# Reloads in the up rounds issued from the scalar engine's queue, and two loops of up rounds written out

## What is computed

```
experts, gates = top-k over two sets of 128 keys, softmax      # 128 experts a position
hdn = gelu(einsum('ted,td->te', expert_down[experts], x))
y   = einsum('te,ted->td', gates * hdn, expert_up[experts])
```

## Time and profile before

| | us |
|---|---|
| median of 3 runs | 3018.91 |
| lowest and highest | 3017.72, 3021.58 |
| the profiled execution: its time | 3036.75 |
| the profiled execution: its span | 3034.7 |

### The profile page before, as it was taken

How to read it: one execution, slowest core, us unless ns; L and a number is a source line. 1 busy time by engine, 2 the same in 40 slices (tenths; PEclk the granted TensorE clock), 3 DMA queues, 4 the chain that set the end, 5 groups by cost and what they waited for, 6 DMA issues and landing times.

```text
span 3034.7 us, 44598 instructions
## 1 busy us (share of the span) xinstructions
PE 2999.1 (99%) x16703; PEld 2676.0 (88%) x16703; DVE 1970.3 (65%) x2549; ACT 1473.1 (49%) x1794; POOL 945.9 (31%) x675
## 2 busy tenths in 40 slices
PE   9999999999999999999999999999999999999998
PEld 8999888888888888998999999999878888888887
DVE  5445564688875555687988976645776555555554
ACT  6445454555564444544444444554555434444443
POOL 3110000088888887155777840000000000000000
PEclk9999999999999999999999999999999999999999
DMA  7764467577777778898999985654446666666664
GB/s 228 246 205 140 147 216 253 187 210 204 213 204 203 225 209 260 296 334 308 351 363 351 349 308 193 191 180 136 132 146 187 192 191 193 191 191 193 190 193 153
DMA packets 227280, 672.30 MB, mean 222 GB/s; under 512 B 57116, under 2 KB 60838, under 8 KB 226737
## 3 DMA queue, kind: packets, MB, share of 16 engines
q1 hardware_dynamic: 157696, 549.79, 55.5%
q0 software_dynamic: 63680, 103.36, 11.8%
q10 hardware_dynamic: 5744, 16.99, 1.5%
HBM read 631.85 MB, written 38.12 MB: 221 GB/s over the span
## 4 chain that ended last, share of the span: by engine, by line
PE 95%; DVE 2%; issue 1%; ACT 1%; DMA 1%; ACTq 0%; SPq 0%; DVEq 0%
PE ps L1954 14%; PE ps L2248 10%; PE ps L2095 8%; PE ps L2097 8%; PE ps L2096 8%; PE ps L1933 8%; PE ps L1934 8%; PE ps L1932 8%; PE ps L1953 7%; PE ps L2247 5%; PE ps L1950 1%; PE ps L2261 1%; PE ps L2260 1%; PE ps L2262 1%; DVE w_lo L691 1%
## 5 line engine op out<-in xcount | busy, mean ns | idle before, releaser
L691 DVE TENSOR_TENSOR w_lo<-raw,w_hi 128x1024 fp32r<-128x1024 f32 (+2 forms) x1072 | 1274.0, 1194 | 855.7 <-ACT w_hi L686 801.1
L686 ACT ACTIVATE w_hi<-raw 128x1024 fp32r<-128x1024 f32 (+2 forms) x1072 | 1107.4, 1034 | 1274.0 <-PE ps L1934 338.4
L1954 PE MATMUL ps<-x_all,w_hi 128*128 128x512 f32 x1920 | 667.7, 390 | 0.0
L1953 PE MATMUL ps<-x_all,w_lo 128*128 128x256 f32 x1920 | 541.7, 282 | 2.3 <-DVE w_lo L691 2.3
L551 POOL DMA_INDIRECT gates<-srch x256 | 486.4, 1900 | 160.5 <-issue 78.5
L2248 PE MATMUL ps<-acts,w_hi 128*128 128x416 f32 x1680 | 514.4, 370 | 3.7 <-issue 3.7
L2247 PE MATMUL ps<-acts,w_lo 128*128 128x208 f32 x1680 | 437.7, 261 | 5.3 <-issue 4.9
L2095 PE MATMUL ps<-w_hi,x_all 128*128 128x440 f32 (+2 forms) x1152 | 436.4, 379 | 0.4 <-DVE w_lo L691 0.4
L1954 PEld LDWEIGHTS ps<-x_all,w_hi 128*128 128x128 f32 x1920 | 360.5, 188 | 74.6
L2096 PE MATMUL ps<-w_lo,x_all 128*128 128x440 f32 (+2 forms) x1152 | 424.7, 369 | 0.0
L2097 PE MATMUL ps<-w_hi,x_all 128*128 128x440 f32 (+2 forms) x1152 | 424.7, 369 | 0.0
(11 more groups left out here) (390 smaller groups left out, 3522.4 us busy)
## 6 DMA issues: line engine op xcount, KB each, us to landing
raw<-in_peer_down SPq DMA_DIRECT2D x256, 512.0 KB
raw<-in_peer_up SPq DMA_DIRECT2D x256, 512.0 KB
raw<-in_w_mlp_in SPq DMA_DIRECT2D x128, 512.0 KB
raw<-in_w_mlp_out SPq DMA_DIRECT2D x128, 512.0 KB
raw<-in_w_in SPq DMA_DIRECT2D x112, 440.0 KB
raw<-in_w_in SPq DMA_DIRECT2D x96, 428.0 KB
raw<-in_w_out SPq DMA_DIRECT2D x64, 512.0 KB
gates<-zero POOLq DMA_DIRECT2D x32, 512.0 KB, 4.9
```

The costliest lines, as they stand in the source:

```text
L686: act.activation(w_hi[:, c % RING, 0:2 * n], raw[:, c % RING, 0:2 * n], ACT.Copy).then_inc(hi_made, 1)
L691: nc.vector.tensor_tensor(w_lo[:, c % RING, 0:2 * n], raw[:, c % RING, 0:2 * n], w_hi[:, c % RING, 0:2 * n].bitcast(F32), ALU.subtract).th ...
L1953: mm(o[:, 0], wl, xh, start=False, stop=False)
L1954: last = mm(o, wh, both, start=False, stop=(k == KT - 1))
```

## The change

GpSimd keeps the reloads of the first four blocks, counted by four new semaphores `first_loaded`. Its other 28 pairs go to ScalarE's queue: `bring_next(nu, g)` is called after the `split_hi` of chunks 9, 11, 13 and 15 of up round nu (block 1, odd chunks) for nu = 0 to 6, and brings block 4(nu + 1) + g. It waits for the same `hid_lo` count, but no longer for `spilled`. GpSimd then has the sets alone, one after the other, held only by `rows_used`; sets 0 to 2 come before its wait for all of `spilled`, as three did. VectorE's `fill` waits for `first_loaded` in its first round and counts one less later. TensorE's and ScalarE's loops over up rounds 1 to 6 become Python loops, so six copies of the body stand in the program. No arithmetic changes.

```diff
-SETS_BY = (3, 7, 15, 22, 29, 36, 44, 48)
...
             def bring(m):
 
-                buf = m % RING
-                if m >= RING:
-                    pool.wait_ge(hid_lo, m - RING + 1)
                 pool.wait_ge(spilled, 16 * (m + 1))
-                pool.dma_start(hid_ring[:, buf].rearrange("p (j s) -> p j s", j=JJ), hid_dense[m, :, :, 0:TD]).then_inc(reloaded[buf], 16)
-                pool.dma_start(gat[:, buf].rearrange("p (j s) -> p j s", j=JJ), gates_dense[m, :, :, 0:TD]).then_inc(gates_loaded[buf], 16)
+                pool.dma_start(hid_ring[:, m].rearrange("p (j s) -> p j s", j=JJ), hid_dense[m, :, :, 0:TD]).then_inc(first_loaded[m], 16)
+                pool.dma_start(gat[:, m].rearrange("p (j s) -> p j s", j=JJ), gates_dense[m, :, :, 0:TD]).then_inc(first_loaded[m], 16)
...
-            done = 0
-            for r in range(PEER_ROUNDS):
-                if r == 1:
-                    pool.wait_ge(pieces_made, 4)
-                    while done < SETS_BY[0]:
-                        gather_rows(done)
-                        done += 1
-                for g in range(RING):
-                    bring(4 * r + g)
-                if r == 1:
+            for m in range(RING):
+                bring(m)
+            pool.wait_ge(pieces_made, 4)
+            for s in range(SETS):
+                if s < GBUF - 1:
+                    gather_rows(s)
+                if s == GBUF - 1:
                     pool.wait_ge(spilled, 16 * 4 * PEER_ROUNDS)
-                    for s in range(done):
-                        gather_hidden(s)
-                while r and done < SETS_BY[r]:
-                    gather_rows(done)
-                    gather_hidden(done)
-                    done += 1
+                    for before in range(s):
+                        gather_hidden(before)
+                if s >= GBUF - 1:
+                    gather_rows(s)
+                    gather_hidden(s)
...
+            def bring_next(nu, g):
+
+                m = 4 * (nu + 1) + g
+                act.wait_ge(hid_lo, m - RING + 1)
+                act.dma_start(hid_ring[:, g].rearrange("p (j s) -> p j s", j=JJ), hid_dense[m, :, :, 0:TD]).then_inc(reloaded[g], 16)
+                act.dma_start(gat[:, g].rearrange("p (j s) -> p j s", j=JJ), gates_dense[m, :, :, 0:TD]).then_inc(gates_loaded[g], 16)
...
+                        if up and i == 1 and c % 2 and nu < PEER_ROUNDS - 1:
+                            bring_next(nu, c // 2)
...
-            with act.Fori(1, PEER_ROUNDS - 1) as r:
+            for r in range(1, PEER_ROUNDS - 1):
                 phase(True, PEER_ROUNDS, r, True, True)
...
-                dve.wait_ge(gates_loaded[g], 16 * (f + 1))
-                dve.wait_ge(reloaded[g], 16 * (f + 1))
+                if f == 0:
+                    dve.wait_ge(first_loaded[g], 32)
+                else:
+                    dve.wait_ge(gates_loaded[g], 16 * f)
+                    dve.wait_ge(reloaded[g], 16 * f)
...
-            up(0)
-            with pe.Fori(1, PEER_ROUNDS - 1) as r:
+            for r in range(PEER_ROUNDS - 1):
                 up(r)
```

More of the change, by code:

```diff
@@ L352, in build @@
         packed, pieces_made, coef_made = sem("packed"), sem("pieces_made"), sem("coef_made")
+        first_loaded = [sem(f"first_loaded{i}") for i in range(RING)]
         gathered = [sem(f"gathered{i}") for i in range(GBUF)]
```

## The result

The changed kernel takes 3040.21 us (median; 3037.79 to 3044.65 over 4 runs), the kernel before 3020.24 us in the same comparison: a ratio of 1.0070, 95% interval 1.0058 to 1.0082, some 20 us slower. The forecast was 3019 us in a range of 3014 to 3030. The profiled execution took 3044.65 us, with a span of 3042.5.

A forecast was written before the change was run, and what follows sets the result against it. The prediction took TensorE's matmuls, filling 99% of the span, to bound the kernel. Its four parts summed as 0 + 0 + 0 + 0 on 3018.91, giving 3019 us, with a range of 3014 to 3030.

The forecast's parts named there:

- What bounds the kernel: Up rounds: TensorE's own pace, 19.29 us a block; no more than 20 us to win in the profiled execution.
- The reading of the crawls: Up rounds: late single matmuls mostly belong to the profiled execution, so about 2 us can be won.
- Part 1: TensorE's up-round loop written out: removing five edges gains 0, 20 more instruction packets cost 0.
- the bound from below: TensorE's instruction packets: rounds 0 and 1 had eight, seven of eight blocks kept 19.29 us, so more cost nothing.
- Rival C: TensorE's instructions come late if a full DMA holds up their packets: 27 us slower, 3046 us; chance 0.04.
- Part 2: ScalarE issues the reloads: 56 at 339 ns, 19.0 us in all, hidden, effect 0.
- The cover of 1.35 us a chunk: ScalarE's wait for TensorE in each chunk of 2.41 us, in which 0.68 us of issues would fit.
- Part 3: GpSimd without reloads: loses 56 issues of 0.75 us and 55.4 us of waits, off the path, effect 0.
- Part 4: Transfers in the reload block: 9.5 MB wanted against 7.5, loads 1.4 MB or 6.4 us short, absorbed, effect 0.
- the reserve of 7.3 us: Slack before TensorE starves: 2.4 us in the loads plus 4.95 us of chunks split ahead, above the 6.4 us shortage.
- Rival A: Loads on SP's queue starve in block 1: 3 to 13 us slower, 3022 to 3032, middle 3027; chance 0.16.
- Rival B: TensorE's crawls are real and vanish when GpSimd's long gather runs end: 20 us faster, 2999 us; chance 0.09.

The follow-up runs named there:

- e11: The kernel before, unchanged, profiled and timed once more; 3018.32 us, ratio 1.0004.
- e9: The kernel before with only TensorE's loop over up rounds written out; 3023.15 us, ratio 1.0026.
- e5: The changed kernel with only one of the four gathers of rows in each set; 3017.32 us, ratio 0.9999 to the kernel before.
- e6: The changed kernel with reload pairs issued behind chunks 3, 7, 11 and 15 of each up round; 3021.01 us, ratio 1.0009 to the kernel before.
- e12: The kernel before with ScalarE's up rounds written out and four junk copies behind chunk 11 of rounds 0 to 6; 3025.63 us, ratio 1.0020.
- e13: The kernel before with the same hold as e12 and only one of the four gathers of rows in each set; 3019.02 us, ratio 0.9998.
- e8: The changed kernel with reloads spread as in e6 and TensorE's loop put back; 3017.38 us, ratio 0.9999 to the kernel before.
- e3: The changed kernel with each reload reading one run of 3328 bytes a partition instead of four of 832; 3039.85 us, ratio 1.0076 to the kernel before.

## Why the prediction was wrong

**What bounds the kernel.** Right: TensorE's pace of 19.29 us a block, in every kernel here. The reading of the crawls, given as not shown, held: e11 has none, and its profiled time is near its median.

**Part 1, the written-out loop of TensorE, taken as 0.** Wrong by 5 to 8 us (e9). The four packets a round are there as forecast, and the edge of the loop indeed costs nothing. The step that failed was the bound from below: that rounds 0 and 1 kept their pace with such packets was read as "they are free". They lost nothing in e9 either, and the loss came in rounds 2 to 6, so these two rounds could not stand for the others; why they are spared was not measured. Rival C's time was wrong too: its late instructions never came; the cost went by way of the loads.

**Part 2, ScalarE's issues, taken as 56 x 0.339 = 19.0 us and hidden.** The count was right, the price was not: 1.89 us in the mean, 106 us in all. Rows 7 priced another shape, one run of 4096 bytes a partition to device memory, issued once a block. Four runs of 832 bytes take 0.55 to 0.65 us in the median when there is room (e5, e6), and up to 7.51 us when there is none. The cover of 1.35 us a chunk was measured well and was too small.

**Part 3, GpSimd.** Right: its sets were in time, with waits for `rows_used` of 93.1 us (79.8 + 13.3) in the changed kernel, and this was worth nothing to TensorE.

**Part 4, the collision.** The shortage was put rather too high: 2.8 MB forecast for the loads, 2.86 to 3.63 measured. The term that failed is the reserve of 7.3 us, against which a shortage of 6.4 us was to cost nothing. Its two parts were counted with room to spare, a transfer that lands in 4.9 us and three split chunks ahead. The first isn't even a load: `gates<-zero` in rows 12 writes to device memory, on GpSimd's queue. And ScalarE's lateness was set against the same 4.95 us in part 2 that the loads' lateness was set against here. Both draw on one store, which refills only while the transfers have room. TensorE starved at shortages of 0.6 to 1.3 MB, 2.6 to 6 us, and in e12 a hold of 4.3 us, of which 1.35 were idle anyway, cost 10.1 us in seven rounds where 4.95 us of reserve should have covered it; in e13, with room, it cost 0.8. The megabytes of a block don't decide alone: with 3.62 MB the block of rows 11 lost nothing, with 3.63 MB block 1 of round 2 lost 3.2 us, as ScalarE was held there too.

**Rival A** came nearest, with a chance of 0.16: TensorE waits for `w_lo` in block 1 of rounds 1 to 6, and in block 2 of some. It was priced at 3 to 13 us of the 20, and its point of 2.9 MB was too low: five of the six rounds starved with more, 3.13 to 3.63 MB. Held issues were missing from it, and so was the clock, which fell to half behind the waits and made block 2 of two rounds longer by 1.6 us. **Rival B** fell: the crawls are missing from this profile and the unprofiled time didn't go down.

## What to carry to other kernels

A reserve of buffered chunks is worth what the transfers can refill: before a move that bunches bytes, compare the megabytes of the busiest block with what a full block moves, and don't count on the reserve when they exceed it. The price of issuing a transfer is taken from one of the same shape at the same fullness, since a long issue holds the engine itself, and here that engine feeds the critical path. Spread over twice the time, the same move cost nothing measurable (e6, and e8 with TensorE's loop kept), and gained nothing, as the kernel before had only some 3 us to win.

## What the runs showed of the hardware

- An issue on ScalarE's queue depends on the runs of the transfer and on the load: 0.34 us for the hidden values in one run a partition (e3), 0.55 in four at the least, up to 7.51 us (the gates) while some 390 GB/s were moving. GpSimd's took 0.75 us before.
- Three busy queues share nearly evenly if their pieces are of like size: 1.80, 1.73 and 1.88 MB in 14 us with pieces of 3.0 to 3.6 KB (e3). With pieces of 832 bytes the third queue got 1.17 MB beside 2.61 and 1.70 in the same stretch of the changed kernel. The Trainium skill (DMA: Bandwidth & Descriptors, Queues, rings and completion order) has each transfer engine take turns between the queues by packet, each of several descriptors. The even thirds of e3 agree with that; how many of the profile's packets make one of those turns, no run here shows.
- 20 more packets of TensorE's instructions, 0.33 MB of some 135 in the same stretch, cost 5 to 8 us where reloads and gathers were bunched (e9), and nothing measurable with a quarter of the gathers (e5) or the reloads spread (e6).
